# 896 streamed columns, two additions a coefficient step, and second-half differences on GpSimd, in the expert layer of a three-layer kernel

## The reference, cut to what matters

```
score_k  = dot(down[e_k], hn)            # row e_k of peer_down, 2048 wide
coef_k   = gate_k * gelu(score_k)
h        = h + sum over k of coef_k * up[e_k]   # row e_k of peer_up, 2048 wide
out      = rmsnorm(h)
```

## Time and profile before

| | us |
|---|---|
| median of 3 runs | 3394.99 |
| lowest and highest | 3392.78, 3398.54 |
| the profiled execution | 3395.3 |
| its span, first to last instruction | 3393.5 |
| gathers of `peer_down`, first to last start | 2084.0 to 2765.6 |
| gathers of `up_rows`, first to last start | 2768.1 to 3365.2 |
| dense multiplications, first to last start | 2938.5 to 3379.7 |
| PE busy, whole span | 2632.1 (78%) |
| DVE busy | 2259.6 (67%) |
| ACT busy | 1013.4 (30%) |
| POOL busy | 827.0 (24%) |

### The profile page before, as it was taken

How to read it: one execution, slowest core, us unless ns; L and a number is a source line. 1 busy time by engine, 2 the same in 40 slices (tenths; PEclk the granted TensorE clock), 3 DMA queues, 4 the chain that set the end, 5 groups by cost and what they waited for, 6 DMA issues and landing times.

```text
span 3393.5 us, 34746 instructions
## 1 busy us (share of the span) xinstructions
PE 2632.1 (78%) x13316; PEld 2068.8 (61%) x13316; DVE 2259.6 (67%) x3026; ACT 1013.4 (30%) x1649; POOL 827.0 (24%) x581
## 2 busy tenths in 40 slices
PE   3789999989989989799997984000098019999998
PEld 3689999977869877798875884000055006544443
DVE  6877777776754455444434458999999984566666
ACT  2233433443444444443334441000087004200000
POOL 5500000000000000000000003733588871345443
PEclk9789999999999999798985987555555555699999
DMA  8768777767856435364330544999999994699998
GB/s 295 258 216 265 266 260 260 250 230 246 286 150 171 134 101 165 100 184 128 114 113 25 174 149 184 377 360 352 345 421 421 422 385 122 217 409 409 409 409 336
DMA packets 340693, 858.35 MB, mean 253 GB/s; under 512 B 38072, under 2 KB 97728, under 8 KB 306864
## 3 DMA queue, kind: packets, MB, share of 16 engines
q1 hardware_dynamic: 265872, 447.54, 39.8%
q0 software_dynamic: 74656, 408.60, 30.9%
HBM read 853.95 MB, written 2.10 MB: 252 GB/s over the span
## 4 chain that ended last, share of the span: by engine, by line
PE 52%; DVE 12%; POOL 8%; issue 3%; ACT 2%; DMA 1%; DVEq 0%; ACTq 0%; POOLq 0%
PE ps L2166 13%; PE ps L1666 10%; PE ps L1668 9%; PE ps L1667 9%; POOL s L625 8%; DVE s L1611 7%; PE ps L2149 2%; PE ps L2127 1%; PE ps L2046 1%; PE ps L2125 1%; PE ps L1927 1%; DMA s<-in_peer_down,s 1%; PE ps L2048 1%; DVE s L1521 0%; DVE s L1512 0%
## 5 line engine op out<-in xcount | busy, mean ns | idle before, releaser
L1666 PE MATMUL ps<-r,r 128*128 128x256 f32 (+2 forms) x3248 | 1065.5, 328 | 81.3 <-DVE r L1044 42.3
L1044 DVE TENSOR_TENSOR r<-s,r 128x1024 fp32r<-128x1024 f32 (+1 forms) x532 | 647.2, 1221 | 616.1 <-ACT r L652 615.6
L1667 PE MATMUL ps<-r,r 128*128 128x256 f32 (+2 forms) x3248 | 1047.2, 322 | 0.0
L1668 PE MATMUL ps<-r,r 128*128 128x256 f32 (+2 forms) x3248 | 1046.3, 322 | 0.0
L652 ACT CAST r<-s 128x1024 fp32r<-128x1024 f32 (+1 forms) x532 | 551.3, 1039 | 954.4 <-PE ps L1668 910.2
L1666 PEld LDWEIGHTS ps<-r,r 128*128 128x128 f32 x3248 | 642.7, 198 | 137.5 <-DVE r L1044 40.3
L1667 PEld LDWEIGHTS ps<-r,r 128*128 128x128 f32 x3248 | 643.1, 198 | 43.6 <-issue 4.6
L1668 PEld LDWEIGHTS ps<-r,r 128*128 128x128 f32 x3248 | 642.0, 198 | 41.0
L1611 DVE CUSTOM_DVE_ANT_0 s<-s,s 128x2048 f32<-128x2048 f32 x256 | 583.8, 2285 | 30.9 <-DMA s<-in_peer_down,s 30.7
L625 POOL DMA_INDIRECT s<-in_peer_down,s x256 | 473.1, 1848 | 448.6 <-DVE s L1569 238.0
L1624 DVE SCALAR_TENSOR_TENSOR s<-s,s,s 128x1024 f32<-128x1024 f32 x256 | 328.6, 1284 | 163.9 <-DMA s<-in_up_rows,s 162.4
(11 more groups left out here) (259 smaller groups left out, 2123.3 us busy)
## 6 DMA issues: line engine op xcount, KB each, us to landing
s<-in_ada_w SPq DMA_DIRECT2D x192, 512.0 KB, 5.4
s<-in_ret_w_in SPq DMA_DIRECT2D x128, 512.0 KB, 5.4
s<-in_up_blocks SPq DMA_DIRECT2D x128, 512.0 KB
s<-in_w_in SPq DMA_DIRECT2D x96, 512.0 KB, 3.7
s<-in_ret_w_in SPq DMA_DIRECT2D x128, 256.0 KB, 3.9
s<-in_ret_w_out SPq DMA_DIRECT2D x64, 512.0 KB, 5.1
s<-in_mla_w_in SPq DMA_DIRECT2D x48, 512.0 KB, 3.7
s<-in_mla_w_out SPq DMA_DIRECT2D x32, 512.0 KB, 3.7
```

Of the source, the lines that this page charges most:

```text
L1044: v.tensor_tensor(lo_of(w), raw_of(w), hi_of(w).bitcast(F), ALU.subtract).then_inc(*lo_made.to(w))
L1666: pe.matmul(o, lh, rh, start=start, stop=False, skip_group_check=True)
L1667: pe.matmul(o, lh, rl, start=False, stop=False, skip_group_check=True)
L1668: return pe.matmul(o, ll, rh, start=False, stop=stop, skip_group_check=True)
```

## The change

DCOL goes from 1024 to 896, so 896 columns are streamed and 1,152 gathered. NU goes from 6 to 5 and NS from 4 to 3, and the buffers change places: two of the block buffers now lie where the chosen numbers (EF) lay, and the first two gather buffers where the selection's scratch lay. So SP waits for `picks_rounded(1)` and `second_copied` before its first block, and GpSimd for `gate_made(1)` before its first gather.

For t = 1 the second-half difference is no longer made by PE. PE turns the second halves of t = 1 once, ACT copies them to SECOND, with the token on the partition, and GpSimd subtracts them from STEP (0 to 127) for four k's at a time, straight into OH2 (`less(q)`). ACT then runs Abs and max(0, 1 - x) on OH2. `compare` for t = 1 makes the first half alone. VectorE runs two additions between two products (behind n = 3, 5, ..., 65).

```diff
-DCOL = 1024
-NU = 6
-NS = 4
+DCOL = 896
+HCOL = DCOL // 2
+NU = 5
+NS = 3
...
             sp.wait_ge(*gate_made.at(1))
+            sp.wait_ge(*picks_rounded.at(1))
+            sp.wait_ge(*second_copied.at(0))
...
+            def less(q):
+
+                g.wait_ge(*built.at(fours[30 + q]))
+                g.tensor_tensor(OH2[q % 2], STEP.unsqueeze(1).broadcast_to([128, 4, 128]),
+                                SECOND[:, 4 * q:4 * q + 4].unsqueeze(2).broadcast_to([128, 4, 128]),
+                                ALU.subtract).then_inc(*second_less.to((1, q)))
+
+            g.wait_ge(*gate_made.at(1))
             for n in range(256):
                 i, t, j = n % NU, n // 128, n % 128
-                if n == 0:
-                    g.wait_ge(*picks_rounded.at(1))
-                elif n == 2:
+                if n == 2:
+                    g.wait_ge(*second_copied.at(0))
+                    g.wait_ge(*d_step.at("all"))
+                    less(0)
+                    less(1)
                     g.wait_ge(*rows_used.at(255))
...
+                if n % 2 == 0 and 2 <= n // 2 - 2 < 32:
+                    less(n // 2 - 2)
...
             for t in range(2):
+                if t:
+                    s.wait_ge(*second_turned.at(0))
+                    s.copy(SECOND, bank[5][:, 0:128]).then_inc(*second_copied.to(0))
...
-                        s.activation(o2, bank[2 + q % 2], ACT.Abs).then_inc(*less_read.to((t, q)))
+                        if t:
+                            s.wait_ge(*second_less.at((1, q)))
+                            s.activation(o2, o2, ACT.Abs).then_inc(*less_read.to((t, q)))
...
-                if 2 <= n < 34:
-                    q = n - 2
+                if n % 2 and n // 2 - 1 in range(32):
+                    q = n // 2 - 1
...
-                for p in range(2):
+                for p in range(2 - t):
...
+                if t:
+                    take(5)
+                    pe.transpose(bank[5][:, 0:128], EF[1][:, 1, :], IDN).then_inc(*second_turned.to(0))
+                    free[5] = second_copied.at(0)
...
-                        r = pe.matmul(bank[2 * t + b], coef_of(t, i2), sbuf[i2 % NS][:, b * 512:(b + 1) * 512],
+                        r = pe.matmul(bank[2 * t + b][:, 0:HCOL], coef_of(t, i2), sbuf[i2 % NS][:, b * HCOL:(b + 1) * HCOL],
```

## The result

The changed kernel takes **3403.6 us** (median of 12 runs, 3394.2 to 3410.4), the kernel before 3394.9 us (12 runs, 3387.0 to 3398.5). The ratio is 1.0026, 95% interval 1.0016 to 1.0036: slower by 0.26%, where 3383 us and a gain were forecast (slower had been given 0.28). The profiled execution took 3403.0 us, with a span of 3401.2 us.

A forecast was written before the change was run, and what follows sets the result against it. Dense stage bounded equally by PE and DMA; PE alone gives nothing. Later dense start +13.5, dense stage -27.6, tail +0.9 make -13.2 us: 3382 from the median, stated as 3383 us, range 3346 to 3413.

The forecast's parts named there:

- What PE leaves free gathers take: Dense stage: gathers use the DMA time PE leaves, with 166.5 MB at 0.409 MB/us giving 407.0 us, 27.6 less.
- no longer a bound: Dense stage: PE needs only 386 us for its multiplications, so it does not bound the stage.
- rival of the starved blocks: Dense stage: three buffers' refills stand behind five gathers, a block every 3.8 us, 456 us instead of 407, 3432; chance 0.09.
- The argument against it: Against starved blocks: q1 got 188 GB/s with both queues full, and blocks need 153.
- The second argument: Dense stage: PE's gaps would not cost the clock, which was 0.95 with PE 44% busy in the first 100 us.
- The coefficient stage: Second token tile: POOL becomes the bound, a step takes 5.1 us instead of 4.60, last difference ends at 2942.4.
- Three issues were to wait for additions: Coefficient stage: two gathers and one difference a step each may wait for a running addition, 6.1 / P us together.
- The start of the dense stage: Dense stage begins at 2952.1, 13.5 us later, about 8.4 us from the last ACT pass as before.
- The prefetch: Gather stage: three smaller blocks loaded ahead instead of four, 0.7 MB less, saving 1.7 us.
- The tail: After the last byte: 21.2 us instead of 20.3, +0.9.
- queue behind GpSimd: Coefficient stage: a difference waits behind two held-up gathers, P is 6.2 and the time 3415; chance 0.18.
- 5.55: Coefficient stage: the step length in us at which the bargain turns.

The follow-up runs named there:

- e8: The changed kernel with four gather buffers instead of five, three block buffers kept: 3406.7 us.
- e1: The changed kernel with four block buffers instead of three, nothing else: 3388.6 us.
- e6: The changed kernel with two block buffers instead of three: 3539.1 us (one run).
- e2: The changed kernel with the second half's equality made on VectorE, without GpSimd's differences and ACT's two passes for them: 3380.0 us.
- e5: The kernel before with two additions a step of the coefficient stage and nothing else changed: 3397.8 us, ratio 1.0008.
- e7: The changed kernel with each of GpSimd's 32 differences made twice: 3447.3 us (one run).
- e12: A repeat of e4, the same kernel: 3360.7 us.
- e4: The changed kernel with both the equality on VectorE and four block buffers: 3361.3 us, ratio 0.9905 to the kernel before.
- e3: The changed kernel with both comparisons on TensorE again, two additions a step and three block buffers kept: 3390.8 us.
- e10: The kernel of e4 with two blocks loaded earlier and 960 streamed columns instead of 896: 3353.4 us.

## Why the prediction was wrong

**The step that failed** is in the dense stage: "What PE leaves free gathers take", with PE's 386 us as "no longer a bound". Gathers did take it, and blocks then came at 3.43 us instead of when they were needed. The stage lasted 432.7 us instead of 407.0. This is the rival of the starved blocks, given 0.09. Its mechanism was right, that two buffers' time doesn't cover a refill, and its sizes were too large. It had a refill of 8.3 us, in a turn behind five queued gathers; e8 shows that their number hardly counts, and the trace has 6.9 us on average from a free buffer to the next block in it. The pace it gave, 3.8 us a block, was 3.43. (By the pace the delay is 7.3, as it counts the short waits of PE within a block; this is worked out from the 3.43 and can't confirm it.) With the gathers through after 400 us, 3.43 us a block make 117 blocks, and 11 more at 3.0 make 433 us, for 432.7 measured; the rival had 456. That the three buffers are the cause is shown by e1: with a fourth one PE never waits from 3000 to 3340 us, and its 128 blocks take 387.1 us.

**Why it was thought unlikely.** The argument against it was q1's 188 GB/s with both queues full; in the dense stage of the changed kernel q1 has 134. Those rows are of a time when four blocks were asked for at once. In the dense stage one block is asked for at a time, each when PE frees its buffer, and a rate that a queue reaches with its work waiting says nothing of how soon a single request lands. The number wanted was from issue to landing, 6.7 us. The kernel before, with four buffers, had 3 x 3.45 = 10.4 us of cover for it; the changed one has 6.0. The second argument, that gaps of PE don't lower its clock, held here, at a granted clock of 1.00. In e6, where the gaps are longer, PE was busy 69% of the time from 3100 to 3200 us and the granted clock was 0.91.

**The coefficient stage** came out close by two errors that cancel. The last difference ended at 2941.4 (2942.4 forecast), and 70 additions were through at the start of the dense stage (71 gathers forecast). The step was 4.77 us, not 5.1. A difference takes 1.09 us on average and not the 1.26 of L606, POOL idles 0.54 us a step instead of 0.70, and the waits fall otherwise than forecast. Three issues were to wait for additions, 1.2 us in all. The difference doesn't wait (1.05 to 1.06 us in 30 of 32); the two gathers do, 1.64 us each on average instead of 0.94, which is 1.4 us in all, so that the sum came out close by luck. The commonest step is 1.05 + 0.16 + 1.88 + 0.31 + 1.21 + 0.02 = 4.63. (The Trainium skill's figure, GPSIMD Engine Reference, section 3.1, gave an estimate of 1.11 us, nearer to the 1.05 than that row.) But the third difference ended at 2801.4 and not at 2794.5. It waits for the builds of step 0, and those wait for a gather of 6.3 us and PE, which the prediction left out. That POOL's gathers are held up by the additions was right: of the 61 gathers of the stage 59 start beside an addition, and each ends 0.81 to 0.82 us after that addition. That the additions are held up by POOL's differences was missed: they average 1.90 us in that stage instead of the forecast 1.43, VectorE is busy 45.8 of 50 us, and e2 shows that this, with POOL's queue and ACT's passes, cost about 24 us in all.

**The start of the dense stage** was 3.3 us late against the forecast. ACT had the last second-half matrix ready at 2942.7, but the last product, which PE needs beside it, stood behind an addition that waited for its gather, and started at 2944.6. The 32 gain multiplications took 7.16 us instead of the 5.06 of before. In the profiled run of before the granted clock was 0.90 and 0.95 from 2932 to 2936 us. In the profiles of the changed kernel and of all twelve experiments, that of e5 with the same work of PE ahead among them, they took 7.2 us. So 2.1 us of the 16.9 between the two starts are that one execution's, and what raised its clock isn't known.

**The prefetch** (-1.7 us) can't be judged. The last dot product of `peer_down` ended at 2784.3 before and 2787.6 after, but over all profiles that point varies from 2776.3 (e8) to 2789.6 (e7), and for one kernel from 2776.6 (e12) to 2785.6 (e4).

**The tail** was forecast behind the last byte, 21.2 us. It lies behind TensorE now, 13.1 us (13.2 before). So the sum: 3.3 at the start, 25.7 in the dense stage, and 8.1 less behind it, make the 20.9 us between the span forecast (3380.3) and the span measured (3401.2).

**The slower rival "queue behind GpSimd"** didn't decide (4.77, under its 5.55), but e7 confirms its price: 1.26 us a step for one more difference, of 1.2 us on average and 0.1 behind it. What the differences cost beside other ways to make them wasn't among the rivals: 23.6 us against VectorE (e2), 12.8 against TensorE (e3). Had the changed kernel kept four block buffers it would have taken 3388.6 (e1), a gain of 0.18% (0.08 to 0.28), 5.6 us above the forecast.

## What to carry to other kernels

Where one buffer less is to pay for something else, cost it by the time from issue to landing of a single transfer under load against the work on the other buffers, not by the rate that its queue can reach. Where two bounds are equal, lowering one gives nothing (e5), and lowering both moves the end to one of the two streams, so look at how far TensorE's end lies behind the last addition: 32 us after the change, -28 with four buffers, -26 in e4, 14 in e10. And before work goes to an idle GpSimd, ask which of VectorE's operations will run beside it.

## What the runs showed of the hardware

- An addition of VectorE on 128x1152 with two SBUF inputs takes 1.42 us. It takes 2.33 to 2.68 us when a 128x512 difference of GpSimd (1.05 us) starts 0.05 to 0.41 us behind its start: so in 25 steps of the changed kernel. It then ends 1.22 to 1.23 us after the difference, wherever that began.
- A gather's instruction on GpSimd takes 0.94 us alone. One that starts beside such an addition ends 0.81 to 0.82 us after the addition (59 of 59 in the changed kernel), and so takes up to 2.1 us, but doesn't lengthen the addition (1.48 us at most in e2).
- A block of 448 or 512 KB lands 6.6 to 6.8 us after its issue (medians) while gathers fill the DMA engines, whether four or five of them are queued, and whether the core moves 373 or 409 GB/s; once the gathers have ended it lands after 3.1 to 3.5 us. From a free buffer to the next multiplication it is 6.9 to 7.1 us on average beside gathers.
- The granted clock stood at 0.90 to 0.95 for 4 us at the end of the coefficient stage in the one profile of the kernel before, and in none of the 13 others did the multiplications there run as fast (7.2 us for 5.1).
- The executions of the changed kernel lie up to 16 us apart (12 runs), those of e8 up to 20 (8 runs), those of e1 within 8 (10 runs). The end of the gather stage alone varies by 13 us over the profiles.
